# Gate and up tiles of a feed-forward pair as seven block products (Strassen's scheme) instead of eight

## What is computed

```python
def swiglu(h, w_gu, w_down):           # h 512x1024, w_gu 1024x5632, w_down 2816x1024
    g, u = jnp.split(h @ w_gu, 2, axis=-1)
    return (jax.nn.silu(g) * u) @ w_down

h = modulate_2(x, norm_g[l, 0], sh1, sc1)
x = x + 0.5 * g1[:, None, :] * swiglu(h, w_ffn1_gu[l], w_ffn1_down[l])
...                                    # attention, x = x + g2 * (...)
h = modulate_2(x, norm_g[l, 2], sh3, sc3)
x = x + 0.5 * g3[:, None, :] * swiglu(h, w_ffn2_gu[l], w_ffn2_down[l])
```

## Time and profile before

| what | value |
|---|---|
| median of 3 runs | 4025.19 us (4024.27 to 4028.97) |
| span of the profiled execution | 4024.5 us |
| PE busy | 3804.0 us, 95% |
| PEld (weight loads, beside PE) | 3013.7 us, 75% |
| VectorE (DVE) busy | 1880.7 us, 47% |
| GpSimd (POOL) busy | 1591.9 us, 40% |
| ScalarE (ACT) busy | 1484.0 us, 37% |
| DMA | 411.94 MB, mean 102 GB/s |

### The profile page before, as it was taken

The page is one execution under the profiler, slowest core; times in us unless marked ns, Lnnn a source line. Parts: engine busy times, 40 slices in busy tenths (PEclk is TensorE's granted clock), DMA queues, the critical chain, the costliest instruction groups (busy, mean ns, idle before and its releaser), DMA issues.

```text
span 4024.5 us, 52248 instructions
## 1 busy us (share of the span) xinstructions
PE 3804.0 (95%) x19172; PEld 3013.7 (75%) x19172; DVE 1880.7 (47%) x3264; ACT 1484.0 (37%) x2301; POOL 1591.9 (40%) x786
## 2 busy tenths in 40 slices
PE   6987899999998889999999999999999999899999
PEld 4875688888775668887888764788878887547887
DVE  3775866453545665664544756322232222452222
ACT  3264532222335653334222564422232224543222
POOL 1221244444331026554555431455555553215554
PEclk9999999999999999999999998999999999999999
DMA  8610134441110016662666220233323333103332
GB/s 252 196 37 19 58 115 131 146 141 59 51 48 19 1 50 216 223 226 87 218 227 209 79 69 11 60 94 98 99 79 99 99 90 86 42 1 92 97 99 74
DMA packets 460500, 411.94 MB, mean 102 GB/s; under 512 B 28095, under 2 KB 405311, under 8 KB 460351
## 3 DMA queue, kind: packets, MB, share of 16 engines
q1 hardware_dynamic: 457903, 408.65, 32.9%
q10 hardware_dynamic: 2448, 1.32, 0.1%
HBM read 406.25 MB, written 7.60 MB: 103 GB/s over the span
## 4 chain that ended last, share of the span: by engine, by line
PE 54%; issue 17%; POOL 13%; DVE 9%; ACT 5%; DMA 1%; POOLq 0%; ACTq 0%; DVEq 0%; SPq 0%
PE psum L239 15%; PE psum L240 14%; PE psum L241 14%; POOL s_wlo L225 10%; PE psum L1645 2%; POOL s_alo L1365 2%; PE psum L1656 1%; PE psum L1633 1%; ACT s_t L1693 1%; PE psum L1624 1%; DVE s_stat L1760 1%; DVE s_t L1770 1%; POOL s_rstd L694 1%; DVE s_h L817 1%; PE psum L160 1%
## 5 line engine op out<-in xcount | busy, mean ns | idle before, releaser
L225 POOL TENSOR_TENSOR s_wlo<-s_raw,s_whi 128x1024 fp32r<-128x1024 f32 x490 | 1181.1, 2418 | 1923.9 <-ACT s_whi L217 1922.5
L239 PE MATMUL psum<-s_xhi,s_whi 128*128 128x512 f32 x3264 | 1228.2, 376 | 22.5 <-POOL s_wlo L225 12.4
L240 PE MATMUL psum<-s_xlo,s_whi 128*128 128x512 f32 x3264 | 1221.4, 374 | 0.0
L241 PE MATMUL psum<-s_xhi,s_wlo 128*128 128x512 f32 x3264 | 1218.3, 373 | 0.0
L217 ACT ACTIVATE s_whi<-s_raw 128x1024 fp32r<-128x1024 f32 x490 | 510.3, 1056 | 1516.0 <-PE psum L241 1511.3
L239 PEld LDWEIGHTS psum<-s_xhi,s_whi 128*128 128x128 f32 x3264 | 616.9, 189 | 143.4 <-issue 15.0
L241 PEld LDWEIGHTS psum<-s_xhi,s_wlo 128*128 128x128 f32 x3264 | 615.5, 189 | 112.4
L240 PEld LDWEIGHTS psum<-s_xlo,s_whi 128*128 128x128 f32 x3264 | 616.7, 189 | 110.4 <-issue 2.4
L239 PE MATMUL psum<-s_ahi,s_whi 128*128 128x512 f32 x1232 | 469.5, 381 | 11.5 <-DVE s_y L1331 7.2
L241 PE MATMUL psum<-s_ahi,s_wlo 128*128 128x512 f32 x1232 | 465.5, 378 | 0.0
L240 PE MATMUL psum<-s_alo,s_whi 128*128 128x512 f32 x1232 | 462.6, 376 | 0.0
(11 more groups left out here) (317 smaller groups left out, 4181.9 us busy)
## 6 DMA issues: line engine op xcount, KB each, us to landing
s_ada_raw<-w_ada SPq DMA_DIRECT2D x224, 512.0 KB, 4.0
s_raw<-w_gu SPq DMA_DIRECT2D x176, 512.0 KB, 3.8
s_raw<-w_up SPq DMA_DIRECT2D x88, 512.0 KB, 4.7
s_raw<-w_dn SPq DMA_DIRECT2D x88, 512.0 KB, 3.5
s_raw<-w_down SPq DMA_DIRECT2D x44, 512.0 KB, 4.6
s_raw<-w_in SPq DMA_DIRECT2D x30, 512.0 KB, 3.9
s_raw<-w_in_ab SPq DMA_DIRECT2D x20, 512.0 KB, 6.3
s_area<-w_first SPq DMA_DIRECT2D x16, 512.0 KB, 11.8
```

The lines of the kernel that those rows point to most:

```text
L225: pool.tensor_tensor(K.wlo[:, c % HL, 0:a * b], K.raw[:, c % RAW, 0:a * b], K.whi[:, c % HL, 0:a * b].bitcast(F32), ALU.subtract).then_inc ...
L239: pe.matmul(out, lh, rh, start=first, stop=False)
L240: pe.matmul(out, lh, rl, start=False, stop=False)
L241: return pe.matmul(out, ll, rh, start=False, stop=last)
```

## The change

The class FastFfn takes the place of Ffn in the four feed-forwards of the second block. Pair 0 is done as before. For the pairs 1 to 21 the gate and up tile are one product of a 2x2 block matrix of weights (two tiles by two halves of the 1024 input features) with a 2x2 block matrix of activations (two halves of the features by two halves of the tokens). Winograd's form of Strassen's scheme makes it of seven block products instead of eight; each is 4 k-steps x 3 matmuls of 128x128 weights by 256 tokens.

- **Activations.** The norm's ScalarE step also writes each tile unrounded (K.xf), and the split x is stored in quarters (quarters()). Four sums of quarters (turned) are made once per feed-forward on VectorE, ScalarE rounds them, and VectorE (three) and GpSimd (one) make their low parts.
- **Weights.** sums() makes four sums of 128x512 blocks of the raw chunks on VectorE for each pair. high() and low() split all seven blocks, each of which has one buffer (self.whi, self.wlo); a block's buffer is free when the same product of the pair before is done. The two raw chunks of a pair are given back together, after low part 6.
- **Products.** product() runs on PE in the order 0 to 6 (FIRST_ORDER in pair 1). Two of the three banks of a pair are written again within the pair, so products 3 to 6 wait for a snapshot (ScalarE) or a combination (VectorE).
- **Combinations.** ScalarE copies product 0 (snap), VectorE makes seven combinations of 256 columns (comb), each with one input in PSUM; silu and the product (gated) then read SBUF.
- The order on VectorE for pair p is: sums of pair p+1, combinations 1 to 7 of pair p, gated. On GpSimd it is: low part 6 of pair p, both down chunks if p is odd, low part 0 of pair p+1, the low part of the activations of pair p-1, low parts 1 to 5 of pair p+1.

```diff
@@ Modulated.high, Modulated.low
-                ins = e.activation(K.xhi[:, k, a:a + w], self.product(k)[:, a:a + w], ACT.Identity,
+                ins = e.activation(self.put(K.xhi, k, a, w), self.like(self.product(k)[:, a:a + w]), ACT.Identity,
                                    bias=K.mod[:, shift:shift + 1])
             ins.then_inc(self.sem["xm_hi"], 1)
+            if self.follower:
+                e.activation(K.xf[:, k, :], self.product(k), ACT.Identity,
...
@@ PreNorm.dve
         self.gains(e, 0)
+        if self.follower:
+            self.follower.sums(e, 1, 0)
         e.wait_ge(self.sem["r0_ready"], self.at("r0_ready", 1))
...
@@ class FastFfn(Ffn)
+    FIRST_ORDER = (0, 5, 3, 1, 2, 4, 6)
+    SETS = (0, 4, None, 1, 5, 2, 3)
+    SUMMED = {2: 1, 4: 2, 1: 3, 5: 4}
+    FIRST_SPLIT = {0: 1, 3: 2, 5: 3, 1: 4, 2: 5, 4: 6}
...
+    def bank(self, p, i):
+        a, b, c = (3, 4, 5) if p % 2 else (2, 0, 1)
+        if p == 1 and i == 2:
+            b_ = 2
+        else:
+            b_ = {0: a, 3: a, 6: a, 1: b, 4: b, 2: c, 5: c}[i]
+        return self.K.pf[:, b_ * BANK:b_ * BANK + TC]
...
+    def sums(self, e, p, n):
+        K, four = self.K, 4 * (p - 1)
+        for c in self.pair_chunks(p):
+            self.raw_there(e, c, n)
+        if p > 1:
+            self.since(e, "f_lo", 6 * (p - 1), n)
+        a11, a12, a21, a22 = [self.raw_half(p, row, k) for row in range(2) for k in range(2)]
+        s1, s2, s3, s4 = [self.sum_tile(i) for i in (2, 1, 4, 5)]
+        e.tensor_tensor(s1, a21, a22, ALU.add).then_inc(self.sem["f_sum"], 1)
+        e.tensor_tensor(s3, a11, a21, ALU.subtract).then_inc(self.sem["f_sum"], 1)
+        self.since(e, "f_sum", four + 1, n)
+        e.tensor_tensor(s2, s1, a11, ALU.subtract).then_inc(self.sem["f_sum"], 1)
+        self.since(e, "f_sum", four + 3, n)
+        e.tensor_tensor(s4, a12, s2, ALU.subtract).then_inc(self.sem["f_sum"], 1)
+    def high(self, e, p, i, n):
+        K = self.K
+        if p > 1:
+            self.since(e, "f_prod", self.done(p - 1, i), n)
+        if i in self.SUMMED:
+            self.since(e, "f_sum", 4 * (p - 1) + self.SUMMED[i], n)
+        else:
+            self.raw_there(e, self.pair_chunks(p)[i == 6], n)
+        ins = e.activation(self.four(self.whi[i]), self.part(p, i), ACT.Copy)
+        if i == 6:
+            ins.then_inc(self.sem["w_hi"], 2)
+        else:
+            ins.then_inc(self.sem["f_hi"], 1)
+    def low(self, e, p, i, n):
+        if i == 6:
+            e.wait_ge(self.sem["w_hi"], self.pair_chunks(p)[1] + 1 + n * LC)
+        else:
+            self.since(e, "f_hi", self.place(p, i), n)
+        ins = e.tensor_tensor(self.four(self.wlo[i]), self.part(p, i), self.four(self.whi[i]).bitcast(F32), ALU.subtract)
+        if i == 6:
+            ins.then_inc(self.sem["w_lo"], 2)
+        else:
+            ins.then_inc(self.sem["f_lo"], 1)
...
+        def product(p, i, n):
+            if i == 6:
+                e.wait_ge(self.sem["w_lo"], self.pair_chunks(p)[1] + 1 + n * LC)
+            else:
+                self.since(e, "f_lo", self.place(p, i), n)
+            if i == 3:
+                self.since(e, "f_snap", p, n)
+            elif i in (4, 6) or i == 5 and p > 1:
+                self.since(e, "f_comb", 7 * (p - 1) + {4: 1, 5: 2, 6: 3}[i], n)
+            hi, lo = self.four(self.whi[i]), self.four(self.wlo[i])
+            xh, xl = [self.four(x) for x in self.x_set(i)]
+            for k in range(4):
+                ins = three(e, self.bank(p, i), (hi[:, k, :], lo[:, k, :]), (xh[:, k, :], xl[:, k, :]),
+                            k == 0, k == 3)
+            ins.then_inc(self.sem["f_prod"], 1)
...
+            for p in (2 * j, 2 * j + 1) if j < GRP else ():
+                if p % 2:
+                    self.since(e, "prod", p - 1, n)
+                for i in range(7):
+                    if p % 2 == 0 and i < 3:
+                        self.since(e, "f_add", 8 * (j - 1) + 6 + i, n)
+                    product(p, i, n)
...
+        def rest(p, n):
+            more = p + 1 < 2 * GRP
+            if more:
+                self.high(e, p + 1, 0, n)
+            rounded(p - 1, n)
+            for i in range(1, 6) if more else ():
+                self.high(e, p + 1, i, n)
+            silu(p, n)
+            for p in (2 * j, 2 * j + 1) if j < GRP else ():
+                self.high(e, p, 6, n)
+                for q in range(2) if p % 2 else ():
+                    self.down_high(e, j, q, n)
+                snap(p, n)
+                rest(p, n)
...
+            if at == 1:
+                self.since(e, "f_snap", p, n)
+                self.since(e, "f_prod", self.done(p, 1), n)
+                out, a, b = s6, first, self.bank(p, 1)
...
+            for p in (2 * j, 2 * j + 1) if j < GRP else ():
+                r = 3 * (p % 2)
+                if p + 1 < 2 * GRP:
+                    self.sums(e, p + 1, n)
+                for at in range(1, 8):
+                    comb(p, at, n)
+                    if ada and at <= 3:
+                        ada.acc(e, j - 1, r + at - 1, n)
+                gated(p, n)
+            for m in range(8):
+                self.since(e, "out_ready", 2 + 8 * (j - 1) + m + 1, n)
+                self.gate.add(K, e, m, self.down_bank(j, m)).then_inc(self.sem["f_add"], 1)
+                if ada and m in (1, 4):
+                    ada.acc(e, j - 1, 6 + m // 4, n)
+            if ada:
...
+        def rest(p, n):
+            more = p + 1 < 2 * GRP
+            if more:
+                self.low(e, p + 1, 0, n)
+            rounded(p - 1, n)
+            for i in range(1, 6) if more else ():
+                self.low(e, p + 1, i, n)
+            for p in (2 * j, 2 * j + 1) if j < GRP else ():
+                self.low(e, p, 6, n)
+                for q in range(2) if p % 2 else ():
+                    split_lo(K, e, self.down_chunk_of(j, q), n)
+                rest(p, n)
...
         for l in range(2):
             m = M2[l]
-            Ffn(K, TX, io["w_gu1"][l], io["w_dn1"][l], DFF, 0, None,
-                [(M2[1] + 8 * g,) for g in range(9)] if l == 0 else [], Gate(m + 16, 0.5))
+            FastFfn(K, io["w_gu1"][l], io["w_dn1"][l],
+                    [(M2[1] + 8 * g,) for g in range(9)] if l == 0 else [], Gate(m + 16, 0.5), before)
             PreNorm(K, (ng2(l, 1), m + 24, m + 32))
             if stop == f"s1_{l}":
                 return finish(K, nc, out)
             mixer2(l, Gate(m + 40, 1.0))
-            PreNorm(K, (ng2(l, 2), m + 48, m + 56))
+            before = PreNorm(K, (ng2(l, 2), m + 48, m + 56), True)
             if stop == f"s2_{l}":
                 return finish(K, nc, out)
-            Ffn(K, TX, io["w_gu2"][l], io["w_dn2"][l], DFF, 0, None, [], Gate(m + 64, 0.5))
+            FastFfn(K, io["w_gu2"][l], io["w_dn2"][l], [], Gate(m + 64, 0.5), before)
             if l == 0:
-                PreNorm(K, (ng2(1, 0), M2[1], M2[1] + 8))
+                before = PreNorm(K, (ng2(1, 0), M2[1], M2[1] + 8), True)
         finish(K, nc, out)
```

More of the change, by code:

```diff
@@ L123, in settled @@
     def settled(self, eng):
-        for s in ("qn_ready", "o_done", "st_done"):
+        for s in ("qn_ready", "o_done", "st_done", "f_add"):
             eng.wait_ge(self.sem[s], self.at(s))
@@ L210, in split_hi @@
 def split_hi(K, act, c, n=0):
-    if c >= len(K.chunks):
+    if c >= len(K.chunks) or c in K.combined:
         return
@@ L415, with put, like @@
 class Modulated(Phase):
+    follower = None
+    def put(self, x, k, a, w):
+        return self.follower.quarters(x, k) if self.follower else x[:, k, a:a + w]
+    def like(self, x):
+        return x.rearrange("p (s t) -> p s t", s=2) if self.follower else x
     def product(self, k):
@@ L458, in low @@
                 k = i - 1
-                e.wait_ge(self.sem["xm_hi"], self.at("xm_hi", k + 1))
+                done = "xf_ready" if self.follower else "xm_hi"
+                e.wait_ge(self.sem[done], self.at(done, k + 1))
                 for s, (a, w) in enumerate(parts(T)):
                     shift = self.pre[s][1] + k
-                    ins = e.scalar_tensor_tensor(out=K.xlo[:, k, a:a + w], in0=self.product(k)[:, a:a + w],
+                    ins = e.scalar_tensor_tensor(out=self.put(K.xlo, k, a, w), in0=self.like(self.product(k)[:, a:a + w]),
                                                  scalar=K.mod[:, shift:shift + 1],
-                                                 in1=K.xhi[:, k, a:a + w].bitcast(F32), op0=ALU.add, op1=ALU.subtract)
+                                                 in1=self.put(K.xhi, k, a, w).bitcast(F32), op0=ALU.add, op1=ALU.subtract)
                 ins.then_inc(self.sem["x_ready"], 1)
@@ L2814, in build @@
     K.nc, K.io, K.total, K.phases, K.chunks, K.ada_tasks, K.steps = nc, io, {}, [], [], 0, 0
-    K.loaded = 0
+    K.loaded, K.combined = 0, set()
     K.ring_now = K.rows = None
@@ L2859, in build @@
             K.alo = sb("alo", [P, 2, 2, T0], F32R, to=ffn)
```

(5 more changed lines are left out.)

304 lines of the change are left out of this document (298 added, 6 removed).

## The result

The changed kernel takes 4320.1 us in the median of 4 runs (4315.3 to 4327.1), against 4024.7 us (4014.2 to 4029.0) for the kernel before on the same chip: a ratio of 1.0736, 95% interval 1.0720 to 1.0752. Slower, by about 295 us; 4300 was forecast. The profiled execution lasts 4325.3 us against 4024.5, and what follows explains those 300.8 us.

The account below looks back on a forecast made before the run. PE was taken to bound the kernel; per feed-forward 14 + 9 x 6.3 - 1.4 = 69 us, 277 for four, on 4024.5 us gave 4302, said as 4300. Its own range was 4210 to 4400, extended down to 4090.

Parts of the forecast that it names:

- What bounds the kernel: Kernel before the change: TensorE (PE) sets the time, busy 95% of the span; the other engines have room.
- Matmuls, 31.4 us a round without stops: Feed-forward rounds: 84 matmuls of 256 columns replace 48 of 512 per pair, gaining 1.4 us a round.
- The even pair's cover of 0.7 us: Even pair: sums run nearly free, combination 1 ends at 5.2 us, product 4 is due at 5.9.
- The odd pair's stop: Odd pair, before product 4: each of four sums waits for a GpSimd step, 9.0 us; PE stands 6.2 us.
- The clock, 1.5 us a stop: After each 6.2 us stop PE restarts at granted clock 0.50, losing 1.5 us, bounds 0 and 3.
- The head, 14 us: Start of each feed-forward: extra copies, turned sums and low parts, late sums of pairs 2 and 3 cost 14 us.
- 6.3 for round 1: Round 1 of each feed-forward, like rounds 1 to 9, was to take 6.3 us more than before.
- The first feed-forward: Feed-forward with modulation sums: taken like the others, its closing modulation step taking 0.3 us of the 0.7 us cover.
- Sum: Whole kernel: 14 + 9 x 6.3 - 1.4 = 69 us per feed-forward, 277 for four, giving 4302, said as 4300.
- Rival 1: Whole kernel: VectorE's sums get through beside GpSimd and PE stays the bound; faster, 3978 us; chance 0.12.
- Rivals 2 to 4: Half waits, 4100 us, chance 0.08; weight loads set pace, 4440, 0.02; change doesn't do what it says, near 4025, 0.02.

Follow-up runs that it names:

- s3_spread: Changed kernel with odd pairs' four sums spread ahead of combination 1 and behind 2, 4 and 6, ScalarE's silu moved earlier; 4093.8 us, ratio 1.0168.
- s1_one_sbuf: Changed kernel, but from pair 2 on each VectorE sum reads its second block from a PSUM bank instead of SBUF; 4067.6 us, ratio 1.0111.
- s2_small_splits: Changed kernel with each down chunk's low part made on GpSimd in two steps of 512 columns instead of one of 1024; 4252.7 us, ratio 1.0573.
- s5_rows_first: Changed kernel with loads of modulation rows 2 to 4 issued ahead of the next pair's weights in the first feed-forward; 4316.5 us, ratio 1.0738.
- (4): Changed kernel with 22 extra matmuls ahead of product 4 of odd pairs 3 to 19, last three feed-forwards; 4266.8 us, ratio 1.0601.

## Why the prediction was right, and where it was off

- **What bounds the kernel**: right. PE had no time to spare, so every wait put ahead of it showed in full.
- **Matmuls, 31.4 us a round without stops**: 31.0. Spacing at 256 columns is 0.118 us in the median of the last loop of s3_spread, a little under the earlier trace rows's 0.120. s1_one_sbuf and s3_spread both show the gain that the change was able to give, 1.8 us a round where 1.4 was worked out.
- **The even pair's cover of 0.7 us**: held, with one of four sums at 1.67.
- **The odd pair's stop, 1.7 + 2.8 + 2.8 + 1.7 = 9.0, PE standing 6.2**: measured 1.77, 2.86, 2.82, 1.65, and 6.19. What the trace of before had left uncertain, that GpSimd gets in between sums that stand back to back, is settled by the rows above and by s2_small_splits.
- **The clock, 1.5 us a stop** (bounds 0 and 3): under-sized, 2.1. The earlier trace rows showed 0.50 for 3.0 us; behind these stops it lasts about 5 (from 4104.82 to some 4110). The round came to 39.3 against 39.1 because the shorter matmuls made up for it.
- **The head, 14 us, with 6.3 for round 1**: 20.3 said, 23.0 measured in the last feed-forward. (The terms as listed there add up to 14.5, not 14.) The waits were nearly right: 2.08 + 1.70 for the turned sums (3.5 said), 1.89 for product 1 of pair 2 (1.9 said), 5.56 for its product 4 (7.5 said; 7.13 in the third feed-forward), 0.8 for the extra copies (1 said), 4.97 in the odd pair of round 1 (6.2 said). Missed was 0.96 ahead of product 4 of pair 1, whose combination stands behind the turned low parts; and the clock was put at 1.4 for one stop, while PE ran at 0.50 behind the stop of 1.89 too (about 3919.0 to 3922.4), and for 6 us behind the one of 5.56. These 9.5 us at half clock lose at most 4.8, as an estimate: some 3 us more than was allowed.
- **The first feed-forward** was taken to be like the others, but for 0.3 us of modulation work in the cover. It lost 77.1 instead of 72.5, and its stop has another make-up: 1.1 to 1.5 us ahead of product 3, ended by the snapshot, and 4.5 ahead of product 4, with sums of 0.68, 1.76, 2.86 and 2.72 us. Left out was SyncE's queue: the modulation rows' loads stand behind the weights', with combined pairs these wait for low part 6, and a row's own buffer comes free only when the row two before it has been read. With the sums' waits gone (s1_one_sbuf) late rows alone left stops of 3.2 to 3.6 us a round there. In the changed kernel the two lay on top of each other and the loss was 4.6 us more than in the last feed-forward; how much of these 4.6 is the queue's isn't shown (s5_rows_first takes the queue place away, and its head and loop are together 2.3 shorter in the profile, which the medians can't tell from nothing). Once the sums were spread, late rows and a full VectorE were the largest loss: s3_spread's 39 us over its expected time, of which the queue place gave back 25. That 69.3 came near 77.1 is in part luck: of the two stops only one had been reasoned out.
- **Sum**: 4 x 69.3 = 277 said, 301 in the profile: 7.8 more in the first feed-forward, 3.2, 2.2 and 3.2 in the others, most of it in the heads, and 7 outside them. In the medians it was 295.
- **Rival 1** (the sums get through, 3978 us) fell with the first row of the odd pair. s1_one_sbuf made it true for three loops by taking the second SBUF input away. The page "Advanced Engine Details and Errata" of the Trainium skill, section "Mode Summary", was cited for it, and the traces speak against reading it so: these are plain sums, and they took up to 2.86 us beside a split. **Rivals 2 to 4** fell too: no two sums passed at once while GpSimd had steps ready, PEld's 74% of the span is overlapped, and the shapes are those of the change.

So the reason is shown and not only argued: taking the shared access away (1), shortening it (2) and moving it off the path (3) each gave back what the theory says, and keeping PE busy (4) priced the clock alone.
